# One encoder step on one core: head 7 as a mixed head too, half of block B ahead of the attended values, kept rows reloaded later

## What is computed

```python
h = rmsnorm(x, g_pre_mix)
z = h @ w_in
b_g, c_g, xin, cq, ckv_raw, kpe_raw, ga, gb = jnp.split(z, [...], axis=-1)
yc, new_buf = short_conv(c_g * xin, conv_buf, conv_w)
y_a = b_g * yc
q = (rmsnorm(cq, g_q) @ w_uq).reshape(B, L, N_HEADS, QK_DIM)
...
y_b = mla_attention(q_nope, q_pe, pos, ckv_all, kpe_all, k_pos, w_uk, w_uv)
merged = jax.nn.sigmoid(ga) * y_a + jax.nn.sigmoid(gb) * y_b
x = x + rmsnorm(merged @ w_o, g_post_mix)
f = jnp.square(jax.nn.relu(rmsnorm(x, g_pre_ffn) @ w1)) @ w2
x = x + rmsnorm(f, g_post_ffn)
```

## Time and profile before

| | |
|---|---|
| median of 3 runs | 1718.98 us |
| lowest and highest | 1718.96 and 1719.39 us |
| the profiled execution's own time | 1719.35 us |
| its span | 1717.5 us |
| PE busy | 1704.5 us, 99% of the span |
| DVE busy | 1313.3 us, 76% |
| ACT busy | 862.5 us, 50% |
| POOL busy | 122.3 us, 7% |
| mean granted clock | 0.998 of full speed |

### The profile page before, as it was taken

How to read it: one execution, slowest core, us unless ns; L and a number is a source line. 1 busy time by engine, 2 the same in 40 slices (tenths; PEclk the granted TensorE clock), 3 DMA queues, 4 the chain that set the end, 5 groups by cost and what they waited for, 6 DMA issues and landing times.

```text
span 1717.5 us, 31904 instructions
## 1 busy us (share of the span) xinstructions
PE 1704.5 (99%) x12735; PEld 1690.0 (98%) x12735; DVE 1313.3 (76%) x2512; ACT 862.5 (50%) x1669; POOL 122.3 (7%) x163
## 2 busy tenths in 40 slices
PE   9999999999999999999999999999999999999997
PEld 9999999999999999999999999999999999999997
DVE  7788877767798777668688788777678887777665
ACT  7636454544554544446366364545446636444452
POOL 1412222122200000000000000000000000000000
PEclk9999999999999999999999999999999999999999
DMA  7888989898842323233133234443433313322231
GB/s 240 199 191 181 230 207 216 188 265 214 175 110 63 111 82 92 87 98 99 62 119 123 90 116 128 116 127 114 162 118 99 99 39 110 99 87 87 74 99 56
DMA packets 85619, 222.09 MB, mean 129 GB/s; under 512 B 9568, under 2 KB 21088, under 8 KB 85472
## 3 DMA queue, kind: packets, MB, share of 16 engines
q1 hardware_dynamic: 66592, 176.01, 32.1%
q0 software_dynamic: 17600, 41.95, 13.8%
q10 hardware_dynamic: 1280, 2.10, 0.4%
HBM read 209.67 MB, written 52.30 MB: 153 GB/s over the span
## 4 chain that ended last, share of the span: by engine, by line
PE 95%; DVE 3%; DMA 1%; issue 1%; ACT 0%; SPq 0%; DVEq 0%; ACTq 0%
PE ring L817 19%; PE ring L819 19%; PE ring L818 19%; PE att L817 11%; PE att L819 11%; PE att L818 11%; DMA w_raw<-blocks_in 1%; PE att L3589 1%; DVE w_lo L2092 1%; PE att L812 1%; PE att L811 1%; PE att L824 0%; PE att L3405 0%; PE att L825 0%; PE att L3744 0%
## 5 line engine op out<-in xcount | busy, mean ns | idle before, releaser
L817 PE MATMUL ring<-xs_hi,w_lo 128*128 128x288 f32 x1872 | 556.5, 297 | 1.2 <-DVE w_lo L2092 0.5
L819 PE MATMUL ring<-xs_hi,w_hi 128*128 128x288 f32 x1872 | 551.5, 295 | 0.0
L818 PE MATMUL ring<-xs_lo,w_hi 128*128 128x288 f32 x1872 | 551.3, 294 | 0.0
L2092 DVE TENSOR_TENSOR w_lo<-w_raw,w_hi 128x1024 fp32r<-128x1024 f32 (+1 forms) x364 | 370.8, 1038 | 38.7 <-ACT w_hi L1209 28.6
L817 PEld LDWEIGHTS ring<-xs_hi,w_lo 128*128 128x128 f32 x1872 | 351.6, 188 | 3.9 <-DVE w_lo L2092 1.3
L818 PEld LDWEIGHTS ring<-xs_lo,w_hi 128*128 128x128 f32 x1872 | 351.8, 188 | 1.4
L819 PEld LDWEIGHTS ring<-xs_hi,w_hi 128*128 128x128 f32 x1872 | 351.6, 188 | 0.0
L819 PE MATMUL att<-f_hi,w_hi 128*128 128x288 f32 x960 | 283.2, 295 | 0.0
L818 PE MATMUL att<-f_lo,w_hi 128*128 128x288 f32 x960 | 282.9, 295 | 0.0
L817 PE MATMUL att<-f_hi,w_lo 128*128 128x288 f32 x960 | 282.6, 294 | 0.0
L817 PEld LDWEIGHTS att<-f_hi,w_lo 128*128 128x128 f32 x960 | 180.4, 188 | 0.0
(11 more groups left out here) (346 smaller groups left out, 3189.9 us busy)
## 6 DMA issues: line engine op xcount, KB each, us to landing
w_raw<-blocks_in SPq DMA_DIRECT2D x197, 512.0 KB, 3.7
weight_sums<-blocks_in POOLq DMA_DIRECT2D x80, 256.0 KB, 7.1
w_raw<-blocks_in SPq DMA_DIRECT2D x58, 256.0 KB, 4.1
weight_sums<-blocks_in POOLq DMA_DIRECT2D x20, 512.0 KB, 5.4
weight_sums<-weight_sums POOLq DMA_DIRECT2D x40, 256.0 KB, 7.6
w_raw<-weight_sums SPq DMA_DIRECT2D x20, 512.0 KB, 4.6
w_raw<-weight_sums SPq DMA_DIRECT2D x40, 256.0 KB, 4.2
small_raw<-small_in SPq DMA_DIRECT2D x16, 320.0 KB, 4.0
```

The lines of the kernel that those rows point to most:

```text
L817: pe.matmul(out, w[1], x[0], start=first, stop=False)
L818: pe.matmul(out, w[0], x[1], start=False, stop=False)
L819: return pe.matmul(out, w[0], x[0], start=False, stop=last)
L2092: return dve.tensor_tensor(out, a, hi.bitcast(F32), ALU.subtract)
```

## The change

**Head 7 becomes a mixed head**, 216 matmuls for 240 in each layer, in an order of its own: products 0 to 3 of the first couple, projections, products 4 to 6, `scores`, products 0 to 3 of the second couple, `turns`, products 4 and 5, the first half of block B, `attended`, the second half of block B, product 6. POOL makes 24 sums for 20. DVE has `last_mixed_head`, ACT a branch of its own.

The diff, cut to its core:

```diff
@@ -82,7 +82,7 @@
-FIRST_MIXED, LAST_MIXED = 2, 6
+FIRST_MIXED, LAST_MIXED = 2, HEADS - 1
...
@@ -91,7 +91,7 @@
-N_EXTRA = 5
+N_EXTRA = 8
...
@@ -173,7 +173,7 @@
-    return pl.my[:, KC - 1, :] if k in (0, HEADS - 1) else pl.rx2[:, :]
+    return pl.my[:, 5, :] if k == 0 else pl.my[:, KC - 1, :] if k == HEADS - 1 else pl.rx2[:, :]
...
@@ -222,16 +222,17 @@
-FIRST_ORDER = [0, 1, 7, 8, 2, 3, 4, 5, 6]
+MIXED_ORDER = {FIRST_MIXED: [0, 1, 7, 8, 2, 3, 4, 5, 6, 9, 10, 11, 12, 13, 14, 15],
...
@@ -934,6 +936,10 @@
+                if h == LAST_MIXED and j > 2:
+                    return ((sum_of(h, 0, 3), half_of(h, 0, 0)), (half_of(h, 0, 1), sum_of(h, 1, 0)),
+                            (sum_of(h, 1, 1), half_of(h, 1, 1)), (sum_of(h, 1, 2), half_of(h, 4, 0)),
+                            (half_of(h, 4, 1), sum_of(h, 1, 3)))[j - 3]
...
@@ -984,28 +991,34 @@
                 if h > 0:
                     sp.wait_ge(pl.merged, L * HEADS + h)
                     sp.dma_start(pl.my_kept[:, h - 1, :], my_row(pl, h - 1)).then_inc(pl.my_stored, 16)
-                if h == HEADS - 1:
-                    sp.wait_ge(pl.my_stored, stored(L, HEADS - 2))
                 for j in range(HEAD_POS[h + 1] - HEAD_POS[h]):
-                    if j == (4 if h == FIRST_MIXED else 3 if is_mixed(h) else 2):
+                    if h < LAST_MIXED and j == (4 if h == FIRST_MIXED else 3 if is_mixed(h) else 2):
                         next_small(h)
-                    if h == HEADS - 1 and j == 2:
+                    if h == LAST_MIXED and j == 2:
+                        sp.wait_ge(pl.projected, L * 40 + 39)
                         sp.dma_start(pl.ctraw[:, :, 0:PAST], cache_t[L]).then_inc(pl.cache_landed, 16)
                         for rows in (slice(0, ROPE), slice(ROPE, P)):
                             sp.dma_start(pl.kcraw[rows, 0:PAST], cache_pe[L]).then_inc(pl.cache_landed, 16)
-                        sp.wait_ge(pl.scored, (L + 1) * HEADS * KT)
-                        sp.dma_start(pl.naraw[:, :, :], cache_n[L]).then_inc(pl.nat_landed, 16)
                     if is_mixed(h):
-                        last = (1, 8, 3, 5, 9, 11, 13, 15) if h == FIRST_MIXED else (1, 3, 5, 8, 9, 11, 13, 15)
+                        last = (1, 8, 3, 5, 9, 11, 13, 15) if h == FIRST_MIXED else \
+                            (1, 3, 5, 9, 11, 13, 8, 15) if h == LAST_MIXED else (1, 3, 5, 8, 9, 11, 13, 15)
+                        if h == LAST_MIXED and j == 6:
+                            sp.wait_ge(pl.ring_full, full(L, r_mixed(h, 14)))
+                            my_load(3)
+                            sp.dma_start(pl.naraw[:, :, :], cache_n[L]).then_inc(pl.nat_landed, 16)
+                            next_small(h)
                         sp.wait_ge(pl.ring_full, full(L, r_mixed(h, last[j])))
                     else:
                         sp.wait_ge(pl.ring_full, full(L, r_hd(h, j, 1)))
                     for q in range(N_HEAD, POSITIONS + N_HEAD):
                         if pos_before(q) == HEAD_POS[h] + j:
                             pos_load(q)
-                    if h == HEADS - 1:
-                        for n in ((0, 1), (2,), (3,), (), ())[j]:
-                            my_load(n)
+                    if h == LAST_MIXED and j == 4:
+                        sp.wait_ge(pl.my_stored, stored(L, HEADS - 2))
+                        my_load(0)
+                    if h == LAST_MIXED and j == 5:
+                        my_load(1)
+                        my_load(2)
             sp.wait_ge(pl.merged, L * HEADS + HEADS)
             for m in range(5, 8):
...
@@ -1645,6 +1652,26 @@
+                if h == LAST_MIXED:
+                    snapshot(0)
+                    pos_hi(L, at + 2)
+                    query_hi(h)
+                    pos_hi(L, at + 3)
+                    keys_hi(h)
+                    pos_hi(L, at + 4)
+                    pos_hi(L, at + 5)
+                    absorbed_hi(h)
+                    conv_started()
+                    snapshot(1)
+                    exponents(h)
+                    pos_hi(L, at + 6)
+                    pos_hi(L, at + 7)
+                    turned_hi(h)
+                    caches_hi()
+                    pos_hi(L, at + 8)
+                    last_gates()
+                    pos_hi(L, at + 9)
+                    return
...
@@ -1673,16 +1700,33 @@
-                if k < HEADS - 1:
-                    eng.wait_ge(pl.my_landed, 64 * (L + 1))
+                if k < 4:
+                    eng.wait_ge(pl.my_landed, 32 * (L + 1))
+                elif k < HEADS - 1:
+                    eng.wait_ge(pl.my_landed_rest, 32 * (L + 1))
-            eng.wait_ge(pl.ring_full, full(L, r_hd(HEADS - 1, 4, 0)))
-            for k in range(HEADS):
+            eng.wait_ge(pl.ring_full, full(L, r_mixed(LAST_MIXED, 7)))
+            for k in range(4):
+            pos_hi(L, POSITIONS + 2)
+            pos_hi(L, POSITIONS + 3)
+            eng.wait_ge(pl.latent_lo, L * 4 + 4)
+            eng.wait_ge(pl.key_lo, L * 2 + 2)
+            apart()
+            for to, src in ((pl.cth, pl.kvh), (pl.ctl, pl.kvl)):
+                act.activation(to[:, :, PAST:NT], src[:, :, NP_:NT].bitcast(F32), ACT.Copy)
+            for to, src in ((pl.kch, pl.keh), (pl.kcl, pl.kel)):
+                ins = act.activation(to[:, PAST:NT], src[:, NP_:NT].bitcast(F32), ACT.Copy)
+            ins.then_inc(pl.cache_new, 1)
+            for k in range(4, HEADS - 1):
+                x_hi_a(k)
+            eng.wait_ge(pl.ring_free, freed(L, r_mixed(LAST_MIXED, 15)))
+            act.activation(pl.gb[:, cols(1)], pl.gb[:, cols(1)], ACT.Tanh, scale=0.5).then_inc(pl.gated, 1)
+            x_hi_a(HEADS - 1)
...
@@ -1729,6 +1773,7 @@
             s_exp(0)
             wo_square(0)
             wo_hi(5)
+            small_hi(L, HEADS)
             wo_square(1)
             wo_square(2)
             s_turned_hi(0)
...
@@ -2774,8 +2812,76 @@
+                def last_mixed_head():
+                    upper_left(0, pl.cv[:, cols(0)])
+                    first_difference(0)
+                    second_sum(0)
+                    pos_lo(L, at + 2)
+                    query_lo(h, 0)
+                    query_lo(h, 1)
+                    pos_lo(L, at + 3)
+                    keys_lo(h)
+                    conv_state(h)
+                    lower_left(0, pl.u[:, 2:2 + NH])
+                    conv_first_half()
+                    lower_right(0, pl.v2[:, :])
+                    upper_right(0, pl.cv[:, cols(1)])
+                    conv_second_half()
+                    pos_lo(L, at + 4)
+                    pos_lo(L, at + 5)
+                    row_maxima(h)
+                    absorbed_lo(h, pl.rest)
+                    upper_left(1, pl.gb[:, cols(0)])
+                    conv_taps(h)
+                    first_difference(1)
+                    probabilities(h)
+                    second_sum(1)
+                    pos_lo(L, at + 6)
+                    pos_lo(L, at + 7)
+                    lower_left(1, pl.ga[:, cols(0)])
+                    turned_lo(h)
+                    lower_right(1, pl.ga[:, cols(1)])
+                    pos_lo(L, at + 8)
+                    src = ready(7)
+                    dve.tensor_tensor(pl.u[:, 0:NH], src, pl.cv[:, 0:NH], ALU.mult).then_inc(pl.ring_free, 1)
+                    eng.wait_ge(pl.gated, of_head(h, 2, 0))
+                    own_freed(7)
+                    own.step(dve.scalar_tensor_tensor(out=pl.ga[:, 0:NH], in0=pl.ga[:, 0:NH], scalar=1.0,
+                                                      in1=pl.u[:, 0:NH], op0=ALU.add, op1=ALU.mult))
+                    pos_lo(L, at + 9)
+                    eng.wait_ge(pl.pv_made, of_head(h, 1, 0))
+                    own.step(dve.scalar_tensor_tensor(out=my_row(pl, h)[:, 0:NH], in0=pl.gb[:, 0:NH], scalar=1.0,
+                                                      in1=pl.att[:, 1024:1024 + NH], op0=ALU.add, op1=ALU.mult))
+                    own.wait()
+                    dve.tensor_tensor(my_row(pl, h)[:, 0:NH], my_row(pl, h)[:, 0:NH], pl.ga[:, 0:NH], ALU.add)                         .then_inc(pl.merged_a, 1)
+                    for k in range(4):
+                        merged_lo(x_part(L, X_WOA + k), k, cols(0))
+                    cache_lo(0, pl.ctl[:, :, 0:PAST], pl.ctraw[:, :, 0:PAST], pl.cth[:, :, 0:PAST])
+                    cache_lo(1, pl.kcl[:, 0:PAST], pl.kcraw[:, 0:PAST], pl.kch[:, 0:PAST])
+                    src = ready(8)
+                    dve.tensor_tensor(pl.u[:, NH:NP_], src[:, 0:NP_ - NH], pl.cv[:, NH:NP_], ALU.mult)
+                    dve.tensor_tensor(pl.u[:, NP_:NT], src[:, NP_ - NH:NH], pl.cv[:, NP_ + 2:NT + 2], ALU.mult)                         .then_inc(pl.ring_free, 1)
+                    pos_lo(L, at + 10)
+                    upper_right(1, pl.gb[:, cols(1)])
+                    own_freed(8)
```

(44 more changed lines are left out.)

116 lines of the change are left out of this document (50 added, 66 removed).

## The result

The changed kernel takes 1729.55 us in the median of 7 runs (1723.66 to 1736.31), the kernel before 1719.39 (1718.96 to 1721.78). The ratio is 1.0056, with a 95% interval of 1.0042 to 1.0070. Forecast were 1718.4 us and a range up to 1722.0; it is slower, outside the range, and the runs spread over 12.7 us where those of before spread over 2.8.

A forecast was written before the change was run, and what follows sets the result against it. PE, busy 1704.5 of 1717.5 us, bounds the whole, at balance with a DVE chain in head 7 and the output projection. Terms -0.75 - 0.3 + 0.4 = -0.65 us give 1718.7, less 0.37 for the median 1718.4; range 1714.8 to 1722.0.

The forecast's parts named there:

- PE's own part: Head 7: 24 matmuls fewer in each layer save 3.18 us, 6.36 us in both.
- The wait ahead of the turned probabilities: Head 7: PE's transposes wait for DVE's late probabilities, about 0.95 us in each layer, bounds 0.6 to 1.2.
- DVE's chain in layer 1: Head 7 to the sample's transposes: DVE's list, with `small` added, leaves a gain of 0.75 us; PE waits 1.5.
- Layer 0, the reload: Head 7: DVE waits 1.1 us for reloaded rows 2 and 3; the sample's transposes come 0.3 us earlier.
- The other half of the path: Layer 0, behind the last merge: `wo5`'s load takes 8.66 us and lies in the chain to the sample's transposes.
- the third rival: Layer 0: a burst of reloads lands rows 2 and 3 after 12 to 13 us, giving 1722.7 us; chance 0.13.
- The feed-forward part, layer 0: First pair behind POOL's four extra sums: weights landing later cost 0 to 2.7 us, taken as 0.4.
- The rule of the Trainium skill: Layer 0's reloads: engines alternating between queue rows would mean 9.8 to 11.8 us; prediction kept 7.4 to 9.5.
- The chances: Whole kernel: faster (under 1715.5 us) 0.18, same 0.69, slower (over 1722.4 us) 0.13.

The follow-up runs named there:

- e12: Changed kernel, rounds from the 14th on in layer 1, `small` prepared behind wo7, head 7's probabilities first and taps behind the first weight block: 1713.18 us, ratio 0.9956.
- e5: Changed kernel with `small` number 8 prepared behind wo7's preparation on ACT and DVE: 1720.99 us, ratio 1.0000.
- e10: Changed kernel with POOL's rounds from the 14th on in layer 1 and `small` number 8 prepared behind wo7: 1714.66 us, ratio 0.9966.
- e2: Changed kernel with nearly all sums of layer 1 (from the 14th round on) held until about 605 us: 1722.13 us, ratio 1.0006.
- e4: Kernel before with its sums of layer 1 (from the 12th round on) held until about 605 us: 1723.47 us, ratio 1.0012.
- e3: Kernel before with four more sums of weights, 24 in all, read by nobody: 1724.59 us, ratio 1.0019.
- e0: Changed kernel run again unaltered, on another chip: 1726.77 us, ratio 1.0036 to the kernel before.
- e1: Changed kernel with POOL's last sums (from the 21st round on) held until about 605 us: 1722.79 us, ratio 1.0013.
- e9: Changed kernel with POOL's rounds from the 14th on made in layer 1, behind the first block of head 0: 1717.89 us, ratio 0.9985.
- e11: Kernel before with its rounds from the 12th on made in layer 1, behind the first block of head 0: 1719.39 us, ratio 0.9993.
- e6: Changed kernel with head 7's probabilities ahead of the convolution's taps and the difference: 1731.41 us, ratio 1.0052.
- e8: Changed kernel, `small` behind wo7, head 7's probabilities first, rounds 14 to 17 held to about 430 us, the rest to about 605: 1721.71 us, ratio 1.0003.

## Why the prediction was wrong, point by point

- **PE's own part**, 3.18 us a layer: right. e12 gets it in layer 1 (3.2 us), once nothing else binds.
- **The wait ahead of the turned probabilities**, 0.95 us a layer: right, 0.9 by the waits, 1.01 by the distance of starts less a pitch.
- **DVE's chain in layer 1**: right in its parts (11.75 us from the maximum to the transposes, -0.7 for the stage, forecast -0.75, a wait of 1.3 to 1.4, forecast 1.5). e5 and e10 show its cause: with `small` out of the chain the wait goes.
- **Layer 0, the reload**: the mechanism was right and a size was off. The term took a landing of 8.2 us, at the low side of the earlier trace rows; it was 10.2, DVE stood for 3.3 us in place of 1.1, and the stage cost +1.9 in place of -0.3. The other half of the path was wrong without harm: `wo5`'s load, taken at 8.66 us, landed in 5.6 and bound nothing (above). The late reload was the third rival, at its near side (it began to cost at 7.1 us, and each us added one). e2 shows that POOL's traffic makes most of the difference: 5.7 us without it. The burst of reloads in one queue, by which the rival explained it, is the smaller part. The four reloads of 360 to 386 us take 7.3 us (median) in the kernel before and 10.6 in the changed one, and without the sums 4.7 (e4) and 5.7 (e2): the burst alone adds 1.0, beside the sums 3.3 in these profiles, and 1.8 against e3's 8.8.
- **The feed-forward part, layer 0**: here the prediction failed. The step is "So the cost is 0 to 2.7 us. I take 0.4". It cost 9.2 us in the first profile and 5.3 in e0's. Three things were wrong in it. It looked at one load, the first pair's, and not at the row of second-matrix loads at 505 to 524 us, where PE stopped first. It took the delay beside POOL as 1.5 to 4.6 us, from the earlier trace rows; the loads came 6.3 us later (10.8 for 4.5, medians). And it had no term for the clock, which was down behind the stop of 4.4 us (0.51 from 527 to 530), 1.4 us. What the runs showed in its place: the sums alone take 3.2 us from the kernel before (e3), and with the last three held back nothing waits from 500 to 700 us (e1). The reason given for the low end, that one sum at a time is a small part of the traffic, was no row: DMA was busy for 0.90 of 520 to 530 us, where it had been 0.23.
- **The rule of the Trainium skill.** The Trainium skill ("DMA: Bandwidth & Descriptors", "Queues, rings and completion order") says that a DMA engine takes turns between the queue rows that have work. The prediction set it aside for the rows 7.4 to 9.5. The reloads' measured 10.6 us for 5.7, 1.9 times, agrees with the double that the prediction drew from it. The weights' 10.8 for 4.5 is 2.4 times, more than that; no run here tells what adds the rest.
- The chances: slower had 0.13, and by the reload alone. Four sums more on a path that weights share were not a rival at all, and should have been.

What stays open is why single runs of the changed kernel lie from 1723.7 to 1736.3 us; only one of these runs has a profile. The granted clock goes with it: its mean is 0.998 in the fastest of the seven runs, 0.997 and 0.996 in the three next, 0.994 and 0.993 in the two at 1732, and 0.991 in the slowest. As an estimate, 0.007 of 1730 us would be up to 12 us, if PE had work all that time. Which stops took it down isn't known. Open as well is why e5's median is 5.8 us below e0's, of which the traces show 2.3, and what in the DMA path makes the loads late beside the sums: the turns between queues, or a path that is full.

## What to carry to other kernels

When a change makes a background engine work longer, list every stage that its traffic now reaches, and the slack of every load in them; the load with the least slack decides. Work that has no hurry belongs where there is slack: the last ten sums cost 8.9 us beside head 7, the output projection and the feed-forward loads of layer 0 (1726.77 for 1717.89 us, e0 and e9, on two chips; by the ratios 8.8) and nothing that shows beside the heads of layer 1, though the loads there are late too. And of a matmul saving on a schedule in balance, ask which other engine's list ends last behind it: here it took the move of one preparation (`small_hi` and `small_lo`, 1.1 us on each engine) and another order of head 7's operations on DVE to turn 1.5 us into 6.2 (e9 and e12, both against e11).

## What the runs showed of the hardware

- A load of 512 KB on SP's queue, issued at 505 to 524 us, takes 4.5 us (median) with POOL idle and 10.8 beside its accumulating DMAs of 256 KB: more than double.
- Behind a stop of PE of 4.4 us the granted clock was at the lower level up to 530 us (0.51 from 527 to 530), 1.4 us of time on top of the stop. The length of a stop alone doesn't decide it: the clock fell as well at a stop of 2.8 us (e6, 0.50 from 421 to 424), of 3.0 (e1, the second of two in layer 0, 0.52 from 421 to 428) and of 3.1 (e8, 0.50 from 523.3 to 526.6), but stayed at 1.00 behind 2.8 us in the changed kernel (419 to 430) and behind 3.5 us in e6 (529 to 532).
- The spread of a kernel's runs went with the place of the sums: 12.7 us for the changed kernel (7 runs), 7.5 for the kernel before beside e1 to e4 (35), and with the late sums in layer 1 1.7 for e9 (11), 1.9 for e11 (11), 2.3 for e10 (5) and 1.0 for e12 (5).
